# GLA first pass: two decay factors per tile computed by ScalarE alone, per head, with the reference as bias

## The chip, the cores and the metric

The kernel runs on one core of a Trainium2 chip. The metric is device time in microseconds of one execution. One execution was profiled; its own time and its span (first to last recorded instruction) are given below, beside the times of the unprofiled runs.

## The reference, cut to what matters

Two layers of a diffusion backbone over 9 tiles of 128 tokens (tile 0 is the context, tiles 1 to 8 the latent tokens), width 1024. Layer 1's mixer is a bidirectional gated linear attention with 4 heads, key width 128, value width 256. With `bc` the running sum of the log gates within a chunk, `S` the state, and everything done once forward and once backward:

```
bc = cumsum(g)                                # g = log_sigmoid(...) / 16
o  = (q * exp(bc)) @ S
o += sum_j<=i  q_i . (exp(bc_i - bc_j) * k_j)  v_j
bl = bc[last]
S  = exp(bl) * S + (k * exp(bl - bc))^T @ v
```

The factor `exp(bl - bc)` decays a token's key from its place to the end of the chunk. The backward direction has its mirror image. The kernel uses whole tiles of 128 tokens as chunks.

## The kernel before, in words

Layer 0, the MLPs and the projections are matrix products on TensorE with weights streamed in and split into two parts; they take nearly all of the span. The change lies in one stage between layer 1's input projection and its output projection: the **GLA first pass**, from about 1659 to 1813 us of the profiled span.

The stage goes through the tiles in the order `TURNS = [0, 8, 7, ..., 1]`; a **turn** is the work for one tile. The program of each engine is written out by hand in a fixed order, and an engine runs its own list strictly in order; semaphores tie the lists together. In a turn the 128x128 attention matrix of each head is built in seven **levels** (half sizes 64, 32, 16, 8, 4, 2, 1). A level needs factors `exp(difference of running sums)`:

- GpSimd (`pool_gla`) writes the differences of a level into one of three `gap` buffers (two subtractions of 128x512, lines 953 and 954; at level 6 two smaller ones).
- ScalarE (`exp_factor`) takes exponentials of it, one for the key side ("S", levels 0 to 5) and one for the query side ("M", all levels), each 128x512 for the four heads at once, into PSUM. Two PSUM banks (`E_BANK`) take the factors in turn, so the exponential of factor m waits until VectorE has used factor m-2.
- VectorE (`scale`, line 2302) multiplies keys or queries by the factor, and `place` (line 2312) puts the finished block of a level's product into the attention matrix `att`.
- TensorE multiplies (`gram`, line 2974), and in levels 2 to 5 makes the output of the turn before (`att_out`, lines 2992 and 2994), one head per level.

Three more factors per tile carry the state: `k1` and `q0` are exponentials of the running sums themselves and need no subtraction. The other two reach to the end of the tile, and these are the ones that the change touches:

- `q1` (query factor of the backward direction, tiles 8 to 1): GpSimd subtracts the tile's total `tot_b` from `bc_b` (line 945), ScalarE takes one 128x512 exponential (line 1542) into PSUM, VectorE multiplies it into `qh`. It comes at the end of a turn: on ScalarE behind `o_take` (line 1589, the copy of the previous tile's output out of PSUM), on VectorE behind `state_step` (line 2324), both of which wait for TensorE's `att_out`.
- `k0` (key factor of the forward direction, tiles 0 to 7): GpSimd subtracts the last column of `bc_f` (line 945), ScalarE takes one 128x512 exponential (`exp_keys`, line 1561) into the SBUF buffer `ek`, and GpSimd multiplies it into the keys in place (`scale_keys`, line 934). For the tile of turn n it is done in level 3 of turn n+1, behind that level's M exponential and ahead of level 4's S exponential. Tile 8 has none, so turn 2 is without it; that of the last turn's tile comes after the last turn.

On GpSimd these two subtractions take a `gap` buffer each, like the levels. `decays` (lines 1525 and 1526) makes `exp(bl)` for all tiles in two small instructions, in turn 0 at level 3.

Of the kernel before, what the change touches and what calls it, by code (L numbers as in the profile page):

```python
# [18 lines left out]
ALU = mybir.AluOpType  # L19
ACT = mybir.ActivationFunctionType  # L20
F32 = mybir.dt.float32
# [4 lines left out]
P = 128  # L26
D = 1024
DC = D // P
TILES = 9
# [14 lines left out]
GH = 4  # L44
# [4 lines left out]
GATE_NORM = 16.0  # L49
# [46 lines left out]
def build(nc, io):  # L96
# [6 lines left out]
    RK = RS + 9248  # L103

    def at(name, shape, dt, offset):
        return nc.alloc_sbuf_tensor_at(name, shape, dt, offset=offset)
# [44 lines left out]
    bc_f = at("bc_f", [P, TILES, GH, P], F32, RA)  # L151
    bc_b = at("bc_b", [P, TILES, GH, P], F32, RC)
# [83 lines left out]
    ek = at("ek", [P, GH, P], F32, RS + 4608)  # L236
    masks = at("masks", [P, len(LEVELS), P], F32, RS)
    tot_b = at("tot_b", [P, TILES, GH], F32, RS + 8704)
    dec = at("dec", [P, 2 * TILES, GH], F32, RS + 8864)
    rs4 = at("rs4", [P, TILES, 2, GH], F32, RK + 6304)  # L240

    k = RK
# [19 lines left out]
    with ExitStack() as ctx:  # L262
# [3 lines left out]
        def sem(name):  # L266
            return ctx.enter_context(nc.semaphore(name))
# [102 lines left out]
        g_sum = sem("g_sum")  # L370
        d_ready = sem("d_ready")
        e_ready = sem("e_ready")
# [27 lines left out]
        ek_ready = sem("ek_ready")  # L400
# [25 lines left out]
        TURNS = [0] + list(range(TILES - 1, 0, -1))  # L426
# [29 lines left out]
        for s in range(UNITS - CONV_UNIT):  # L456
            late_burst = s // 3 % 3 == 2
            last = s >= UNITS - CONV_UNIT - 3
# [396 lines left out]
        def key_order():  # L855

            return [tile for tile in TURNS if tile < TILES - 1]

        def factor_order():

            out = []
            for a, tile in enumerate(TURNS):
                for level in range(NL):
                    if LEVELS[level] > 1:
                        out.append(("S", tile, level))
                    out.append(("M", tile, level))
                    if level == 1 and a:
                        out += closing(TURNS[a - 1])
                    if level == 2 and tile != 1:
                        out.append(("k1", tile, 0))  # L870
                if tile:
                    out.append(("q1", tile, 0))
            return out + closing(TURNS[-1])

        factor_at = {x: i for i, x in enumerate(factor_order())}
        FACTORS = len(factor_at)

        def gap_order():

            out = []  # L880
            for a, tile in enumerate(TURNS):
                for level in range(NL):
                    out.append(("g", tile, level))
                    if level == 3 and a and TURNS[a - 1] in key_order():
                        out.append(("k0", TURNS[a - 1], 0))
                if tile:
                    out.append(("q1", tile, 0))
            out.append(("k0", TURNS[-1], 0))
            return out

        gap_at = {x: i for i, x in enumerate(gap_order())}

        def gap_user(kind, tile, level):
            if kind == "k0":
                return ek_ready, key_order().index(tile) + 1
            return e_ready, factor_at[("M" if kind == "g" else kind, tile, level)] + 1

        def gap_of(r):

            return gap[r % len(gap)]  # L900

        def plain(x):

            return x[:, 0:2, :].rearrange("p u (h n) -> p (u h) n", n=P)

        def halves(t, level):

# [17 lines left out]
        def pool_gla(pool):  # L925
            pool.wait_ge(g_sum, 2 * GH)
            pool.wait_ge(pan_used, SLOTS + FEEDS_TO_GLA - 2)
            gaps = gap_order()
            def scale_keys(tile):

                n = key_order().index(tile)
                pool.wait_ge(ek_ready, n + 1)
                pool.wait_ge(gram_ready, 8 * (TURNS.index(tile) + 1))
                nc.gpsimd.tensor_tensor(gk[:, tile], gk[:, tile], ek[:], ALU.mult).then_inc(k0_ready, 1)

            for r, (kind, tile, level) in enumerate(gaps):
                if kind == "g" and level == 6 and TURNS.index(tile) and TURNS[TURNS.index(tile) - 1] in key_order():
                    scale_keys(TURNS[TURNS.index(tile) - 1])
                if r >= len(gap):
                    pool.wait_ge(*gap_user(*gaps[r - len(gap)]))  # L940
                out = gap_of(r)
                if kind in ("k0", "q1"):
                    b = bc_b if kind == "q1" else bc_f
                    ref = tot_b[:, tile].unsqueeze(2) if kind == "q1" else b[:, tile, :, P - 1:P]
                    nc.gpsimd.tensor_tensor(plain(out), b[:, tile], ref.broadcast_to([P, GH, P]), ALU.subtract).then_inc(d_ready, 1)
                    continue
                n = LEVELS[level]
                f, b = halves(bc_f[:, tile], level), halves(bc_b[:, tile], level)
                f_ref, b_ref = f[:, :, 0, n - 1:n], b[:, :, 1, 0:1]
                x = out[:, :, :].rearrange("p u (b n) -> p b u n", n=n)  # L950
                if n > 1:
                    f_ref, b_ref = (y.unsqueeze(3).broadcast_to(f.shape) for y in (f_ref, b_ref))
                    nc.gpsimd.tensor_tensor(x[:, :, 0::2], f, f_ref, ALU.subtract)
                    nc.gpsimd.tensor_tensor(x[:, :, 1::2], b_ref, b, ALU.subtract).then_inc(d_ready, 1)
                else:
                    nc.gpsimd.tensor_tensor(x[:, :, 1, :], b_ref, b[:, :, 0, :], ALU.subtract)
                    nc.gpsimd.tensor_tensor(x[:, :, 2, :], f[:, :, 1, :], f_ref, ALU.subtract).then_inc(d_ready, 1)
            scale_keys(TURNS[-1])
# [42 lines left out]
        def _(act):  # L1001
# [11 lines left out]
            def own(ins):  # L1013
                ins.then_inc(act_own, 1)
                act.wait_ge(act_own, T.next(act_own))
# [145 lines left out]
            for u in range(UNITS):  # L1161
                p, n = divmod(u, GROUPS)
# [263 lines left out]
            for part in range(2 * 4):  # L1426
                p = part % 4
# [4 lines left out]
                g, amid, after = TURNED[part]  # L1432
# [86 lines left out]
            v_take(GROUPS - 1)  # L1519
            values_taken = [T.last(acc_read[t]) for t in range(GT)]  # L1520

            def decays():

                act.wait_ge(g_sum, 2 * GH)
                nc.scalar.activation(dec[:, 0:TILES, :], bc_f[:, :, :, P - 1], ACT.Exp, scale=1 / GATE_NORM)
                nc.scalar.activation(dec[:, TILES:2 * TILES, :], tot_b[:], ACT.Exp, scale=1 / GATE_NORM).then_inc(dec_ready, 1)

            def exp_factor(kind, tile, level=0):

                m = factor_at[(kind, tile, level)]  # L1530
                if m >= 2:
                    act.wait_ge(xt_ready, m - 1)
                else:
                    act.wait_ge(acc_read[(0, GT - 1)[m]], values_taken[(0, GT - 1)[m]])
                s = 1 / GATE_NORM
                out = factor(m)
                if kind in ("k1", "q0"):
                    nc.scalar.activation(out, (bc_b if kind == "k1" else bc_f)[:, tile], ACT.Exp, scale=s).then_inc(e_ready, 1)
                elif kind == "q1":
                    r = gap_at[(kind, tile, 0)]  # L1540
                    act.wait_ge(d_ready, r + 1)
                    nc.scalar.activation(out, plain(gap_of(r)), ACT.Exp, scale=-s).then_inc(e_ready, 1)
                else:
                    r = gap_at[("g", tile, level)]
                    act.wait_ge(d_ready, r + 1)
                    n = LEVELS[level]
                    x = gap_of(r)[:, 0::3, :] if kind == "S" else gap_of(r)[:, 1:3, :]
                    y = out.rearrange("p h (b s n) -> p s (h b) n", s=2, n=n)
                    nc.scalar.activation(y, x.rearrange("p s (b n) -> p s b n", n=n), ACT.Exp,  # L1549
                                         scale=-s if kind == "S" else s).then_inc(e_ready, 1)  # L1550

            def exp_keys(tile):

                n, r = key_order().index(tile), gap_at[("k0", tile, 0)]
                if n == 0:
                    for i in range(2):
                        act.wait_ge(og_out[i], 16 * ((TILES + 1 - i) // 2))
                else:
                    act.wait_ge(k0_ready, n)
                act.wait_ge(d_ready, r + 1)  # L1560
                nc.scalar.activation(ek[:], plain(gap_of(r)), ACT.Exp, scale=-1 / GATE_NORM).then_inc(ek_ready, 1)

            def place_wide(a, level):

# [26 lines left out]
            for a, tile in enumerate(TURNS):  # L1591
                for level in range(NL):
# [3 lines left out]
                    if level == 0:  # L1596
                        if a >= 2:
# [3 lines left out]
                                             scale=2.0).then_inc(diag_ready, 1)  # L1601
# [1517 lines left out]
```

## Time and profile before

| | us |
|---|---|
| median of 3 runs | 2732.11 |
| lowest, highest | 2731.95, 2733.51 |
| the profiled execution's own time | 2731.22 |
| its span | 2729.4 |
| TensorE busy | 2616.1 (96%) |
| VectorE busy | 1758.6 (64%) |
| ScalarE busy | 1373.6 (50%) |
| GpSimd busy | 195.6 (7%), nearly all of it in this stage |

The page's 40 slices of 68 us show TensorE at nine tenths or more in almost all of them; in the slices of the GLA stage it is at eight. The shares over the whole span say little on this stage, so it is read by itself: by windows, by GpSimd's groups of instructions, and by each engine's instructions in order of time. In the views, "idle before" is the time in which an engine stood still ahead of an instruction, with what released it. Neighbouring instructions of one form are merged in a timeline row (x2, x4). An instruction's duration is longer than its distance to the next, since two on one engine overlap a little.

### The profile page before, as it was taken

The page shows a single profiled execution, that of the slowest core. Times are in us where ns is not written, and L with a number is a line of the kernel's source. Part 1 is how long each engine was busy: PE and PEld are TensorE (multiplying, and loading weights), DVE is VectorE, ACT ScalarE, POOL GpSimd, SP SyncE. Part 2 cuts the span into 40 slices and gives each one's busy share as a digit, 9 for nine tenths or more (in the row PEclk, how much of TensorE's full clock was granted, in tenths as well). Part 3 has the DMA queues.
Part 4 walks back from the last instruction along what each step waited for, and adds up shares of the span by engine and source line. Part 5 has one row for each costly group of instructions (what it writes and reads, how often), then busy time and mean ns, then how long its engine had stood idle before and what let it go on. Part 6 is the DMA issues. An engine that isn't in the chain of part 4 may idle for free.

```text
span 2729.4 us, 37797 instructions
## 1 busy us (share of the span) xinstructions
PE 2616.1 (96%) x14547; PEld 2298.4 (84%) x14547; DVE 1758.6 (64%) x2814; ACT 1373.6 (50%) x2382; POOL 195.6 (7%) x180
## 2 busy tenths in 40 slices
PE   5999999999999999999999998889999999999998
PEld 3878888789998999788898887777899989998886
DVE  4146666564557777779822457985645577876787
ACT  5134445554444555554622677765544445554444
POOL 0000000000000000000000006982000000000000
PEclk9999999999999999999999999999999999999999
DMA  7643232644443554756523451015344444556565
GB/s 279 208 150 108 86 108 63 192 116 124 124 124 112 189 165 151 241 154 222 155 70 95 147 166 56 10 55 188 126 123 122 122 129 148 180 170 215 178 208 191
DMA packets 268606, 393.82 MB, mean 144 GB/s; under 512 B 25830, under 2 KB 207532, under 8 KB 267404
## 3 DMA queue, kind: packets, MB, share of 16 engines
q1 hardware_dynamic: 262192, 373.68, 43.5%
q10 hardware_dynamic: 4220, 9.86, 1.0%
q0 software_dynamic: 2016, 7.86, 0.8%
q8 instruction: 116, 1.90, 0.3%
q14 instruction: 62, 0.51, 0.1%
HBM read 331.98 MB, written 59.38 MB: 143 GB/s over the span
## 4 chain that ended last, share of the span: by engine, by line
PE 82%; DVE 7%; ACT 5%; DMA 3%; issue 2%; SPq 1%; POOL 1%; ACTq 0%; DVEq 0%; POOLq 0%
PE ps L2666 21%; PE ps L2779 15%; PE ps L2835 15%; PE ps L2744 9%; PE ps L2480 8%; PE ps L2870 4%; PE ps L2441 2%; PE ps L2534 2%; PE ps L2561 1%; PE ps L2497 1%; PE ps L2974 1%; ACT prT L1131 1%; SPq L659 1%; DVE t_g L1888 1%; ACT ps L1549 1%
## 5 line engine op out<-in xcount | busy, mean ns | idle before, releaser
L1693 DVE TENSOR_TENSOR p_lo<-p_raw,p_hi 128x1024 fp32r<-128x1024 f32 (+1 forms) x299 | 367.3, 1232 | 338.7 <-ACT p_hi L1042 332.4
L1042 ACT ACTIVATE p_hi<-p_raw 128x1024 fp32r<-128x1024 f32 x267 | 280.2, 1053 | 222.8 <-DMA p_raw<-mlp_w 116.2
L2835 PE MATMUL ps<-p_hi,hq_hi 128*128 128x512 f32 x672 | 209.3, 392 | 11.2 <-DVE c_sum L2046 4.6
L2835 PE MATMUL ps<-p_hi,hq_lo 128*128 128x512 f32 x672 | 207.1, 389 | 0.0
L2835 PE MATMUL ps<-p_lo,hq_hi 128*128 128x512 f32 x672 | 207.1, 389 | 0.0
L2779 PE MATMUL ps<-t_hi,w_hi 128*128 128x384 f32 x512 | 172.5, 337 | 11.1 <-DVE c_sum L2046 11.1
L2779 PE MATMUL ps<-t_hi,w_lo 128*128 128x384 f32 x512 | 172.4, 337 | 0.0
L2779 PE MATMUL ps<-t_lo,w_hi 128*128 128x384 f32 x512 | 172.2, 336 | 0.0
L2744 PE MATMUL ps<-hm_hi,p_lo 128*128 128x384 f32 x512 | 172.0, 336 | 0.0
L2744 PE MATMUL ps<-hm_hi,p_hi 128*128 128x384 f32 x512 | 171.7, 335 | 0.0
L2744 PE MATMUL ps<-hm_lo,p_hi 128*128 128x384 f32 x512 | 171.5, 335 | 0.0
L1330 ACT ACTIVATE hq_hi<-hq_raw 128x768 fp32r<-128x768 f32 x112 | 94.5, 844 | 137.7 <-DMA hq_raw<-hid_scratch 137.5
L2480 PE MATMUL ps<-h_hi,p_hi 128*128 128x384 f32 x432 | 158.5, 367 | 3.9 <-DVE h_lo L1714 3.9
L2835 PEld LDWEIGHTS ps<-p_hi,hq_hi 128*128 128x128 f32 x672 | 124.4, 188 | 41.3 <-issue 7.8
L2835 PEld LDWEIGHTS ps<-p_lo,hq_hi 128*128 128x128 f32 x672 | 126.1, 188 | 26.5
L2835 PEld LDWEIGHTS ps<-p_hi,hq_lo 128*128 128x128 f32 x672 | 126.1, 188 | 26.4
L2081 DVE TENSOR_TENSOR hq_lo<-hq_raw,hq_hi 128x768 fp32r<-128x768 f32 x112 | 107.0, 955 | 61.2 <-ACT hq_hi L1330 61.1
L2480 PE MATMUL ps<-h_hi,p_lo 128*128 128x384 f32 x432 | 145.3, 336 | 0.0
L2480 PE MATMUL ps<-h_lo,p_hi 128*128 128x384 f32 x432 | 144.9, 335 | 0.0
L2030 DVE TENSOR_TENSOR w_lo<-w_pair,w_hi 128x512 fp32r<-128x512 f32 x128 | 87.4, 685 | 65.4 <-ACT w_hi L1300 65.4
L2666 PE MATMUL ps<-p_hi,hid_hi 128*128 128x512 f32 x384 | 122.6, 400 | 3.3 <-DVE p_lo L1693 3.3
L1257 ACT ACTIVATE relu<-ps 128x384 f32<-128x384 f32 x64 | 31.5, 492 | 182.5 <-PE ps L2744 182.5
(326 smaller groups left out, 6435.8 us busy)
## 6 DMA issues: line engine op xcount, KB each, us to landing
p_raw<-mlp_w SPq DMA_DIRECT2D x208, 512.0 KB, 3.8
hq_raw<-hid_scratch SPq DMA_DIRECT2D x112, 384.0 KB, 4.2
mod_p<-mod_w SPq DMA_DIRECT2D x80, 512.0 KB, 4.0
w_pair<-mlp_w SPq DMA_DIRECT2D x32, 1024.0 KB, 5.8
p_raw<-gla_w_in SPq DMA_DIRECT2D x56, 512.0 KB, 3.5
hid_scratch<-c_out SPq DMA_DIRECT2D x128, 192.0 KB, 1.9
hid_scratch<-s_out SPq DMA_DIRECT2D x96, 192.0 KB, 2.0
p_raw<-gla_w_out SPq DMA_DIRECT2D x24, 512.0 KB, 3.6
```

What stands on the lines that cost most here:

```text
L1042: nc.scalar.activation(p_hi[s][:, :, 0:width], p_raw[s][:, :, 0:width], ACT.Copy).then_inc(pan_hi, 1)
L1330: nc.scalar.activation(hq_hi[layer][n % 4][:], hq_raw[layer][n % 4][:], ACT.Copy).then_inc(hq_rounded, 1)
L1693: V.tensor_tensor(p_lo[s][:, :, 0:width], p_raw[s][:, :, 0:width], p_hi[s][:, :, 0:width].bitcast(F32), ALU.subtract).then_inc(pan_lo, 1)
L2030: V.tensor_tensor(w_lo[layer][i][:], raw_piece(j, step), w_hi[layer][i][:].bitcast(F32), ALU.subtract).then_inc(piece_lo, 1)
L2081: V.tensor_tensor(hq_lo[layer][i][:], hq_raw[layer][i][:], hq_hi[layer][i][:].bitcast(F32), ALU.subtract).then_inc(hq_ready, 1)
L2441: return M.transpose(out, in_, ident[0:n, 0:n])
L2480: mm = M.matmul(ps[:, b, 0:GN], w[s][:, c, :], h0[n][x][:, c, :], start=(c == 0 and x == 0 and w is p_hi), stop=(c == DC - 1 and w is p_lo))
L2666: mm = M.matmul(acc(slot)[:, cols], x, flat(w[s])[:, cols], start=begin and edge == 0, stop=end and edge == 2)
L2744: mm = M.matmul(ps[:, b, 0:GN], w[s][:, c, :], x[:, c, :], start=(c == 0 and x is hi and w is p_hi), stop=(c == DC - 1 and w is p_lo))
L2779: mm = M.matmul(ps[:, c_bank(j, which), 0:GN], w[layer][i][:, c, :], second_operand(layer, step, x, c), start=(step < 3 and c == 0 and x = ...
L2835: mm = M.matmul(acc(t)[:, 512 * to:512 * (to + 1)], x[layer][n % 4][:, half, t * P:(t + 1) * P], flat(w[s])[:, 512 * half:512 * (half + 1) ...
L2870: mm = M.matmul(ps[0:width, b, 0:GN], w[s][:, c, 0:width], hx[g][x][:, c, :], start=(c == 0 and x == 0 and w is p_hi), stop=(c == DC - 1 a ...
```

## The change

The two differences disappear from GpSimd's list (and with them their turns in the ring of `gap` buffers). ScalarE reads the running sums directly and takes the exponential of each head by itself (128x128), with the reference divided by 16 as a per-partition bias. The biases stand in a small new tile `last_gap`, filled by two Copy activations and one wait of ScalarE for itself, ahead of its first exponential of the stage. So each `q1` and each `k0` factor is now four ScalarE instructions in place of one. `decays` no longer has its own wait, since the new instructions wait for the same thing earlier.

```diff
--- before.py
+++ after.py
@@ -237,6 +237,7 @@
     masks = at("masks", [P, len(LEVELS), P], F32, RS)
     tot_b = at("tot_b", [P, TILES, GH], F32, RS + 8704)
     dec = at("dec", [P, 2 * TILES, GH], F32, RS + 8864)
+    last_gap = at("last_gap", [P, 2, TILES, GH], F32, RK + 5152)
     rs4 = at("rs4", [P, TILES, 2, GH], F32, RK + 6304)
 
     k = RK
@@ -881,27 +882,16 @@
             for a, tile in enumerate(TURNS):
                 for level in range(NL):
                     out.append(("g", tile, level))
-                    if level == 3 and a and TURNS[a - 1] in key_order():
-                        out.append(("k0", TURNS[a - 1], 0))
-                if tile:
-                    out.append(("q1", tile, 0))
-            out.append(("k0", TURNS[-1], 0))
             return out
 
         gap_at = {x: i for i, x in enumerate(gap_order())}
 
         def gap_user(kind, tile, level):
-            if kind == "k0":
-                return ek_ready, key_order().index(tile) + 1
-            return e_ready, factor_at[("M" if kind == "g" else kind, tile, level)] + 1
+            return e_ready, factor_at[("M", tile, level)] + 1
 
         def gap_of(r):
 
             return gap[r % len(gap)]
-
-        def plain(x):
-
-            return x[:, 0:2, :].rearrange("p u (h n) -> p (u h) n", n=P)
 
         def halves(t, level):
 
@@ -939,11 +929,6 @@
                 if r >= len(gap):
                     pool.wait_ge(*gap_user(*gaps[r - len(gap)]))
                 out = gap_of(r)
-                if kind in ("k0", "q1"):
-                    b = bc_b if kind == "q1" else bc_f
-                    ref = tot_b[:, tile].unsqueeze(2) if kind == "q1" else b[:, tile, :, P - 1:P]
-                    nc.gpsimd.tensor_tensor(plain(out), b[:, tile], ref.broadcast_to([P, GH, P]), ALU.subtract).then_inc(d_ready, 1)
-                    continue
                 n = LEVELS[level]
                 f, b = halves(bc_f[:, tile], level), halves(bc_b[:, tile], level)
                 f_ref, b_ref = f[:, :, 0, n - 1:n], b[:, :, 1, 0:1]
@@ -1519,9 +1504,12 @@
             v_take(GROUPS - 1)
             values_taken = [T.last(acc_read[t]) for t in range(GT)]
 
+            act.wait_ge(g_sum, 2 * GH)
+            nc.scalar.activation(last_gap[:, 0], bc_f[:, :, :, P - 1], ACT.Copy, scale=1 / GATE_NORM)
+            own(nc.scalar.activation(last_gap[:, 1], tot_b[:], ACT.Copy, scale=1 / GATE_NORM))
+
             def decays():
 
-                act.wait_ge(g_sum, 2 * GH)
                 nc.scalar.activation(dec[:, 0:TILES, :], bc_f[:, :, :, P - 1], ACT.Exp, scale=1 / GATE_NORM)
                 nc.scalar.activation(dec[:, TILES:2 * TILES, :], tot_b[:], ACT.Exp, scale=1 / GATE_NORM).then_inc(dec_ready, 1)
 
@@ -1537,9 +1525,10 @@
                 if kind in ("k1", "q0"):
                     nc.scalar.activation(out, (bc_b if kind == "k1" else bc_f)[:, tile], ACT.Exp, scale=s).then_inc(e_ready, 1)
                 elif kind == "q1":
-                    r = gap_at[(kind, tile, 0)]
-                    act.wait_ge(d_ready, r + 1)
-                    nc.scalar.activation(out, plain(gap_of(r)), ACT.Exp, scale=-s).then_inc(e_ready, 1)
+                    for h in range(GH):
+                        last = nc.scalar.activation(out[:, h, :], bc_b[:, tile, h, :], ACT.Exp, scale=-s,
+                                                    bias=last_gap[:, 1, tile, h:h + 1])
+                    last.then_inc(e_ready, 1)
                 else:
                     r = gap_at[("g", tile, level)]
                     act.wait_ge(d_ready, r + 1)
@@ -1551,14 +1540,16 @@
 
             def exp_keys(tile):
 
-                n, r = key_order().index(tile), gap_at[("k0", tile, 0)]
+                n = key_order().index(tile)
                 if n == 0:
                     for i in range(2):
                         act.wait_ge(og_out[i], 16 * ((TILES + 1 - i) // 2))
                 else:
                     act.wait_ge(k0_ready, n)
-                act.wait_ge(d_ready, r + 1)
-                nc.scalar.activation(ek[:], plain(gap_of(r)), ACT.Exp, scale=-1 / GATE_NORM).then_inc(ek_ready, 1)
+                for h in range(GH):
+                    last = nc.scalar.activation(ek[:, h, :], bc_f[:, tile, h, :], ACT.Exp, scale=-1 / GATE_NORM,
+                                                bias=last_gap[:, 0, tile, h:h + 1])
+                last.then_inc(ek_ready, 1)
 
             def place_wide(a, level):
```

## Rows read from the trace of the kernel before

**Rows 1.** The page, section 4: shares of the span in the chain by engine.

```profile
PE 82%; DVE 7%; ACT 5%; DMA 3%; issue 2%; SPq 1%; POOL 1%; ACTq 0%; DVEq 0%; POOLq 0%
```

**Rows 2.** Windows: stretch, us; busy (count) PE, PEld, DVE, ACT, POOL; clock; DMA share, GB/s.

```profile
1758.90:1775.50 16.60, 13.61 (x95) 11.83 (x94) 15.64 (x27) 12.08 (x23) 16.60 (x18) 1.00 0.00 1
1780.00:1784.00 4.00, 3.95 (x17) 3.62 (x18) 3.26 (x5) 3.59 (x9) 4.00 (x5) 0.57 0.00 0
```

**Rows 3.** GpSimd groups by line: count, busy us, mean ns, idle before and its releaser.

```profile
L934 POOL TENSOR_TENSOR gk<-gk,ek 128x512 f32<-128x512 f32 x8 | 10.2, 1278 | 1.9 <-ACT ek L1561 1.9
L945 POOL TENSOR_TENSOR gap<-bc_f 128x512 f32<-128x512 f32 x8 | 8.3, 1042 | 1.0 <-ACT ps L1549 1.0
```

**Rows 4.** VectorE in order of time: start us, us, line, operation, idle before.

```profile
1694.60 0.69 DVE L2302 TENSOR_TENSOR qh<-gq,ps 128x512 f32<-128x512 f32 x1
...
1706.51 0.70 DVE L2302 TENSOR_TENSOR xx<-gq,ps 128x512 f32<-128x512 f32 x1
...
1711.02 0.69 DVE L2302 TENSOR_TENSOR qh<-gq,ps 128x512 f32<-128x512 f32 x1
...
1719.30 0.69 DVE L2302 TENSOR_TENSOR xx<-gq,ps 128x512 f32<-128x512 f32 x1
...
1720.54 0.67 DVE L2302 TENSOR_TENSOR xx<-gk,ps 128x512 f32<-128x512 f32 x1
...
1722.95 0.67 DVE L2302 TENSOR_TENSOR xx<-gq,ps 128x512 f32<-128x512 f32 x1
...
1725.74 1.65 DVE L2324 SCALAR_TENSOR_TENSOR st<-st,dec,ps 128x256 f32<-128x256 f32 x4
1727.43 0.69 DVE L2302 TENSOR_TENSOR qh<-gq,ps 128x512 f32<-128x512 f32 x1
...
1777.22 0.69 DVE L2302 TENSOR_TENSOR qh<-gq,ps 128x512 f32<-128x512 f32 x1
...
1784.64 0.74 DVE L2312 COPY_PREDICATED att<-masks,ps 128x512 f32<-128x512 int32 x1 [1.17 <-PE ps L2974]
...
1794.73 0.69 DVE L2302 TENSOR_TENSOR qh<-gq,ps 128x512 f32<-128x512 f32 x1
...
1811.32 0.69 DVE L2302 TENSOR_TENSOR qh<-gq,ps 128x512 f32<-128x512 f32 x1
```

**Rows 5.** ScalarE in order of time, the same columns.

```profile
1664.51 1.11 ACT L1549 ACTIVATE ps<-gap 128x512 f32<-128x512 f32 x2
...
1718.66 0.60 ACT L1549 ACTIVATE ps<-gap 128x512 f32<-128x512 f32 x1 [0.42 <-DVE kh L2302]
1719.29 0.63 ACT L1561 ACTIVATE ek<-gap 128x512 f32<-128x512 f32 x1
1719.83 1.10 ACT L1549 ACTIVATE ps<-gap 128x512 f32<-128x512 f32 x2
...
1725.74 1.02 ACT L1589 ACTIVATE o_b<-ps 128x1024 f32<-128x1024 f32 x1 [1.29 <-PE ps L2994]
1726.66 0.60 ACT L1542 ACTIVATE ps<-gap 128x512 f32<-128x512 f32 x1
```

**Rows 6.** ScalarE in order of time, in the attention of layer 0.

```profile
162.16 0.37 ACT L1120 ACTIVATE prob<-ps,smx 128x128 f32<-128x128 f32 x1 [1.97 <-DVE smx L1812]
162.43 0.19 ACT L1120 ACTIVATION_READ_ACCUMULATOR prob<-ps,smx 128x1 f32 x1
```

**Rows 7.** ScalarE's groups of instructions, the shapes kept apart.

```profile
L1034 ACT ACTIVATE h<-ps,mods 128x128 f32<-128x128 f32 x32 | 14.7, 458 | 38.4 <-PE ps L2441 36.9 <-DVE mods L1735 1.2 <-DVE h_lo L1714 0.3
...
L1123 ACT ACTIVATE smx<-sink,smx 128x1 f32<-128x1 f32 x72 | 20.3, 283 | 0.0
...
L1138 ACT ACTIVATE q_t<-ps 128x128 f32<-128x128 f32 x36 | 9.6, 266 | 1.2 <-PE ps L2561 1.1
...
L1120 ACT ACTIVATE prob<-ps,smx 128x128 f32<-128x128 f32 x8 | 2.9, 362 | 11.5 <-DVE smx L1812 11.5
```

**Rows 8.** The same view, 1655 to 1840 us.

```profile
L1525 ACT ACTIVATE dec<-bc_f 128x36 f32<-128x36 f32 x1 | 0.3, 263 | 0.0
```

## The prediction

> **What bounds the kernel now.** I read the chain by engine first: TensorE holds 82% of it and GpSimd 1% [rows 1]. That is a mean over stages, and in this stage it misleads, so I went on to busy time by window. In the stretch 1758.90 to 1775.50, one turn of the GLA first pass, GpSimd is busy for 16.60 of 16.60 us, VectorE for 15.64, TensorE for 13.61, ScalarE for 12.08 [rows 2]. By that view GpSimd sets the pace and the change takes the right load off. Third, the engines in order of time, to see what the pace would be without GpSimd. I measure a turn from VectorE's multiplication into `qh` (the q1 factor in use) to the next one. The marks [rows 4] give 16.42 for turn 2 (1694.60 to 1711.02), 16.41 for turn 3 (to 1727.43), 49.79 for turns 4 to 6 (to 1777.22, so 16.60 each), 17.51 for turn 7 and 16.59 for turn 8. Turn 2 has neither a k0 subtraction (1.04) nor a key multiplication (1.28) on GpSimd [rows 3]: GpSimd has some 16.60 - 1.04 - 1.28 = 14.3 us of work there, and the turn still took 16.42. So a second bound lies only 0.2 us under GpSimd's: the ring of ScalarE and VectorE, which hand each factor over two PSUM banks. Turn 3 shows it twice:
>
> - From `qh` to the M multiplication of level 5: 1722.95 - 1711.02 = 11.93 (turn 2: 1706.51 - 1694.60 = 11.91) [rows 4].
> - From there to the next `qh`: 1727.43 - 1722.95 = 4.48 [rows 4]. TensorE's `att_out` ends 2.79 after that multiplication, and releases both `o_take` on ScalarE and the state step on VectorE (both start at 1725.74) [rows 4, 5]. On VectorE the state step takes 1.69 to `qh`. On ScalarE q1's exponential starts 0.92 after `o_take` (1726.66), 3.71 after the multiplication, and its user could start 0.64 later: that is the distance from exponential to user in level 3, 1718.66 to 1719.30 [rows 4, 5]. So 3.71 + 0.64 = 4.35, under 4.48 by 0.13 only.
>
> **Part 1, GpSimd.** Each tile loses up to two subtractions of 1.04 us [rows 3], 2.1 us of 16.60 in a full turn. What this can give back is the distance to the ring's pace, 16.60 - 16.41 = 0.19 us a turn; it stands inside the sum below, since that builds new turns from turn 3's pieces, in which GpSimd costs 0.3 or less.
>
> **Part 2, the price of a small exponential.** The nearest row is the 128x128 exponential of layer 0's attention, with a per-partition bias: 362 ns [rows 7]. Its single instance lasts 0.37, and the next instruction starts 0.27 after it [rows 6]; an overlap of about 0.09. q1 goes to PSUM and I take 0.36 long, 0.27 apart. k0 goes from SBUF to SBUF: the one-element exponential with bias between SBUF tiles takes 283 ns [rows 7], and 127 more elements at (362 - 283) / 127 would add only 0.08, but that row and this differ in where they read. Where both rows exist, 512-wide exponentials take 0.63 to SBUF and 0.60 to PSUM [rows 5], so k0 gets 0.03 more: 0.39 long, 0.30 apart. Bounds: below, 266 ns, a 128x128 copy without a pointer operand [rows 7], about 0.175 apart; above, 458 ns with two pointer operands [rows 7], about 0.37 apart.
>
> The Trainium skill ("ScalarE: Activation LUTs", What ACT_TABLE_LOAD costs) says that a [128,1] pointer bias makes an activation about 280 ns + 0.833 ns per column and that neighbours overlap by about 93 ns, so four heads pay the fixed part four times: 0.387 long and 0.294 apart for 128 columns, by which the sum below would be about 8.0 instead of 7.3 (q1 0.10 more in 8 turns, k0 0.02 less in 7). The row with 0.362 stands a little under it, and I go by the row.
>
> **Part 3, k0 in level 3 (turns 1 and 3 to 8).** Before: level 3's M exponential starts at 1718.66, `ek` at 1719.29, level 4's S exponential at 1719.83, 0.54 after `ek` [rows 5]. Its user starts at 1720.54 [rows 4]; 0.64 after the exponential would be 1720.47, so the slack is 0.07. New: 4 x 0.30 = 1.20 instead of 0.54, and 1.20 - 0.54 - 0.07 = **0.59** of it delays VectorE. Behind `ek` on ScalarE stand all the later exponentials; VectorE waits for level 4's S factor, TensorE for VectorE. Nothing takes it back, as VectorE's list up to level 5 is already back to back.
>
> **Part 4, q1 at a turn's end (turns 1 to 8).** The first small exponential starts at the same 3.71. The last starts 3 x 0.27 = 0.81 later, lasts 0.36, plus 0.04 to the user: 3.71 + 1.21 = 4.92 against 4.48, **0.44** more. Next turn's S exponential starts at 3.71 + 4 x 0.27 = 4.79, its user could go at 5.43, and VectorE is at 4.92 + 0.60 anyway: no further loss.
>
> **Part 5, the first turn.** ScalarE makes the two small biases between its copy of the last value panel and the first exponential (1664.51 [rows 5]), when three gap buffers have long been filled and everyone waits for ScalarE. An instruction of this size takes 263 ns [rows 8]: about 0.17 to the next, 0.22 for the second, 0.05 for the wait on its own result: **0.44**, nothing hides it. Bounds 0.3 and 0.6.
>
> **The sum.** A full turn becomes 11.93 + 0.59 + 4.92 = 17.44. GpSimd needs 14.5 in it, so it is no bound even where `scale_keys` now gets `ek` 0.7 later. Turn 2 has no k0: 11.91 + 4.92 = 16.83. In turn 7 TensorE's granted clock was 0.57 over four microseconds [rows 2], and the placement at 1784.64 waited 1.17 for it [rows 4]; I keep 1.12 for one such drop. Turns 2 to 8: 16.83 + 6 x 17.44 + 1.12 = 122.59, against 1811.32 - 1694.60 = 116.72 [rows 4], so +5.87. Turn 1 has both places at turn 3's prices: 0.59 + 0.44 = 1.03. The first turn 0.44. Together **+7.3 us**. After the last turn k0's exponentials for tile 1 come behind q1, but TensorE first makes half of the last output; no cost. The second pass and the output projection start from the end of this stage and are shifted as a whole. Against the profiled execution, 2731.2 (span 2729.4 and 1.8 around it), that is 2738.6. The median of the runs is 0.9 above that execution: **2739.5**.
>
> With the lower price: k0 4 x 0.175 - 0.54 - 0.07 = 0.09; q1 3.71 + 3 x 0.175 + 0.27 + 0.04 = 4.54, 0.06 more. Turns 2 to 8 take 16.45 + 6 x 16.56 + 1.12 = 116.9, +0.2; with turn 1 and the start +0.8. With the upper price (k0 0.87, q1 3.71 + 1.61 = 5.32) it is +12.5.
>
> **Rivals.**
>
> - GpSimd is the only bound (turns of 16.60 with no idle time on it speak for that; turns 2 and 3 against it). Then every turn falls as far as VectorE's busy time, 15.64: 7 x 15.64 + 1.12 = 110.6, -6.1, with 0.44 at the start -5.7: 2726.4. It decides as soon as the small exponentials lie in idle time of ScalarE, of which a turn has 16.60 - 12.08 = 4.5 us. Chance 0.07.
> - The pointer operand costs nothing much and heads overlap as in the lower bound: +0.8, 2732.9. Against it: both rows with a bias are dearer than the copy. Chance 0.10.
> - Only q1 is on the path, k0 is absorbed (VectorE's later wait for TensorE or GpSimd eats it): 7.3 - 7 x 0.59 = +3.2, 2735.3. For it: turns 4 to 6 are 0.19 longer than turn 3, so some slack exists; against it, level 4's user follows without a gap. Chance 0.15.
> - Longer turns leave TensorE idle for longer at each turn's end, and its clock is granted at the lower level more often than the once of turn 7. At 1.1 us for each, two to four more give +9.5 to +11.7: 2742.7. Chance 0.13.
>
> **How the numbers follow.** The forecast has the remaining 0.55: 5.5 to 9 us more (2737.6 to 2741), by prices between 0.26 and 0.30 apart and one clock drop fewer or more. A measurement of this kernel tells some 0.2%, 5.5 us, from no change. Slower by more: the forecast (0.55), the clock rival (0.13), less a little for a low price: 0.66. Faster by more: half of the first rival's case, where the gain is nearly whole, and a little for what I don't see: 0.05. Within it: 0.29. The range leaves out the first rival and the far end of the clock's: 2732.5 to 2743.5.
>
> **What would show each step.** In the trace after: GpSimd idle for about 2.9 us of each turn, before level 6's gap (it waits for `ek`) and for free buffers; eight small exponentials per turn, 0.27 to 0.30 apart; the distance between level 3's M user and level 4's S user 1.83 (1.24 before); level 5's M user to `qh` 4.92 with VectorE idle before `qh` for ScalarE, and the state step still starting with `o_take`; turns of 17.4. The prediction is wrong if VectorE shows no idle time ahead of `qh` and of level 4's S user, or if turns come out under 16.4.

## The result and the profile after

| | us |
|---|---|
| before, median of 7 runs on the same chip (lowest, highest) | 2732.11 (2730.67, 2733.91) |
| after, median of 7 runs | 2743.29 (2740.65, 2745.4) |
| ratio after to before, 95% interval | 1.004 [1.003, 1.0049] |
| the profiled execution after: time, span | 2741.89, 2740.1 |
| after once more on another occasion (6 runs) against 22 runs of before: medians | 2740.96, 2731.76 |
| ratio there | 1.0033 [1.0021, 1.0044] |

The change makes the kernel slower, by 9 to 11 us. The forecast was 2739.5, or +7.4, with a range of 2732.5 to 2743.5; the first result lies 0.2 under the upper end of that range.

One turn after the change by window (columns as in [rows 2]): turn 4, from `qh` to `qh`.

```profile
1731.41:1748.94 17.53, 13.79 (x94) 11.92 (x94) 15.85 (x26) 13.45 (x29) 14.71 (x16) 1.00 0.00 1
```

It takes 17.53 us where the turn of [rows 2] took 16.60. GpSimd, busy for all of 16.60 then, is now idle for 2.8 us; ScalarE went from 12.08 to 13.45. No engine is full, and the turn is longer. The same turn on VectorE shows where the time sits:

```profile
1731.41 0.69 DVE L2293 TENSOR_TENSOR qh<-gq,ps 128x512 f32<-128x512 f32 x1 [0.59 <-DVE st L2315]
...
1739.69 0.69 DVE L2293 TENSOR_TENSOR xx<-gq,ps 128x512 f32<-128x512 f32 x1
...
1741.48 0.69 DVE L2293 TENSOR_TENSOR xx<-gk,ps 128x512 f32<-128x512 f32 x1 [0.46 <-ACT ps L1538]
...
1743.90 0.68 DVE L2293 TENSOR_TENSOR xx<-gq,ps 128x512 f32<-128x512 f32 x1
...
1746.70 1.66 DVE L2315 SCALAR_TENSOR_TENSOR st<-st,dec,ps 128x256 f32<-128x256 f32 x4
1748.94 0.69 DVE L2293 TENSOR_TENSOR qh<-gq,ps 128x512 f32<-128x512 f32 x1 [0.58 <-DVE st L2315]
```

Against turn 3 in [rows 4]: from level 3's M user (1739.69) to level 4's S user (1741.48) it is 1.79 in place of 1.24, with 0.46 idle for ScalarE; from level 5's M user (1743.90) to `qh` (1748.94) 5.04 in place of 4.48. The state step still starts with the output copy (1746.70 in both views), and `qh` comes 0.58 behind it; the view names the state step as releaser, but that had ended. It is the exponential on ScalarE:

```profile
1739.06 0.60 ACT L1538 ACTIVATE ps<-gap 128x512 f32<-128x512 f32 x1 [0.43 <-DVE kh L2293]
1739.69 1.28 ACT L1550 ACTIVATE ek<-bc_f,last_gap 128x128 f32<-128x128 f32 x4
1740.87 1.10 ACT L1538 ACTIVATE ps<-gap 128x512 f32<-128x512 f32 x2
...
1746.70 1.02 ACT L1580 ACTIVATE o_b<-ps 128x1024 f32<-128x1024 f32 x1 [2.08 <-PE ps L2985]
1747.62 1.23 ACT L1529 ACTIVATE ps<-bc_b,last_gap 128x128 f32<-128x128 f32 x4
```

This is the same turn on ScalarE, the answer to [rows 5]. `ek` now holds the engine for 1.18 (1739.69 to 1740.87) instead of 0.54, and q1's last exponential ends at 1748.85, 0.09 before `qh`. The small exponentials by form, after:

```profile
L1550 ACT ACTIVATE ek<-bc_f,last_gap 128x128 f32<-128x128 f32 x32 | 10.2, 389 | 0.2
L1529 ACT ACTIVATE ps<-bc_b,last_gap 128x128 f32<-128x128 f32 x32 | 9.9, 360 | 0.0
```

GpSimd's wait ahead of its key multiplication, in level 3 to 4 of turn 3, where it had none in full turns before:

```profile
1723.50 1.27 POOL L924 TENSOR_TENSOR gk<-gk,ek 128x512 f32<-128x512 f32 x1 [1.98 <-ACT ek L1550]
```

And the first turn: the two biases between the last value copy and the first exponential, which starts 1.33 after that copy began.

```profile
1664.17 1.02 ACT L1443 ACTIVATE gv<-ps 128x1024 f32<-128x1024 f32 x1 [0.33 <-PE ps L2657]
1665.09 0.26 ACT L1508 ACTIVATE last_gap<-bc_f 128x36 f32<-128x36 f32 x1
1665.24 0.22 ACT L1509 ACTIVATE last_gap<-tot_b 128x36 f32<-128x36 f32 x1
1665.50 1.12 ACT L1538 ACTIVATE ps<-gap 128x512 f32<-128x512 f32 x2
```

**Where the 10.7 us between the two profiled executions lie.** I lined up TensorE's 14547 matmuls, which are the same in both, one by one. The stage begins 0.58 later (drift of the long stage before it, which the change doesn't touch), and ends 9.65 later. From there to the end the distance varies between 7.8 and 10.9, with single stretches of lower clock in one or the other, and the spans differ by 10.7. Inside the stage: 0.41 at the start, 1.34 to the first `qh`, and turns 2 to 8 of 16.95, 17.53, 17.53, 18.43, 18.55, 17.52 and 17.54, together 124.05 against 116.72 [rows 4], so 7.33; in all 9.08. The 1.34 hold the two delays once (0.56 and 0.59) and 0.19 more in a part where both profiles show the clock at its lower level twice. Three of these turns, 5, 6 and 8, hold a drop of TensorE's granted clock (a short stretch at the lower of its two levels), which makes each 0.9 to 1.05 us longer; before, one did (turn 7, 17.51, 0.91 above the 16.60 of turns 4 to 6). One of them in the windows of the kernel after:

```profile
1752.00:1756.00 4.00, 4.00 (x21) 3.70 (x21) 3.04 (x5) 3.60 (x8) 3.95 (x5) 0.62 0.00 0
```

### The profile page after: what moved, and what is told of

Read it like the earlier page. It is cut to its first block, busy times and chain, and to the rows that moved or that the text cites. A ratio compares the mean times of both kernels' runs of the same rounds, so it can differ in the third digit from the quotient of the medians.

```text
span 2740.1 us, 37816 instructions
## 1 busy us (share of the span) xinstructions
PE 2618.3 (96%) x14547; PEld 2301.6 (84%) x14547; DVE 1759.7 (64%) x2814; ACT 1385.0 (51%) x2432; POOL 181.0 (7%) x164
## 4 chain that ended last, share of the span: by engine, by line
PE 81%; DVE 7%; ACT 5%; DMA 3%; issue 3%; SPq 1%; POOL 0%; ACTq 0%; DVEq 0%
PE ps L2657 21%; PE ps L2770 15%; PE ps L2826 14%; PE ps L2735 9%; PE ps L2471 8%; PE ps L2861 4%; PE ps L2432 2%; PE ps L2525 2%; PE ps L2552 1%; PE ps L2965 1%; PE ps L2488 1%; DMA hq_raw<-hid_scratch 1%; SPq L660 1%; ACT prT L1116 1%; DVE t_g L1879 1%
```

## The experiments

All were run with the kernel before on the same chip. "Before" is 2732.41 (33 runs) for the first four, 2732.45 (22) for the next three, 2731.76 (22) for the last three. Drops of the clock are told apart from turns by reading full turns without one.

**e1, the k0 half alone.** The kernel before with

```diff
-    gap_order: ("k0", tile, 0)
-    activation(ek[:], plain(gap_of(r)), ACT.Exp, scale=-1 / GATE_NORM)
+    for h in range(GH): activation(ek[:, h, :], bc_f[:, tile, h, :], ACT.Exp, scale=-1 / GATE_NORM, bias=last_gap[...])
```

> The kernel before, with only the k0 half of the change: GpSimd's k0 subtraction gone, four small exponentials in level 3. The theory (ScalarE and VectorE pass factors in a ring, and longer blocks on ScalarE lengthen it): distance from level 3's M user to level 4's S user 1.79 in place of 1.24, distance from level 5's M user to qh 4.48 as before, so a turn of 16.95, and +3 to +4 us in all. Rival (GpSimd is the bound): its work falls to 15.6 a turn, the turns fall with it, about -6 us. Second rival (the halves only hurt together): no change.

Measured: 2734.35, ratio 1.0011 [1.0002, 1.002]; turn 2 (no k0) 16.39, full turns 16.96 to 17.00. VectorE in one of them:

```profile
1753.65 0.69 DVE L2305 TENSOR_TENSOR xx<-gq,ps 128x512 f32<-128x512 f32 x1
...
1755.44 0.69 DVE L2305 TENSOR_TENSOR xx<-gk,ps 128x512 f32<-128x512 f32 x1 [0.46 <-ACT ps L1550]
...
1757.86 0.69 DVE L2305 TENSOR_TENSOR xx<-gq,ps 128x512 f32<-128x512 f32 x1
...
1760.67 1.66 DVE L2327 SCALAR_TENSOR_TENSOR st<-st,dec,ps 128x256 f32<-128x256 f32 x4
1762.36 0.69 DVE L2305 TENSOR_TENSOR qh<-gq,ps 128x512 f32<-128x512 f32 x1
```

1.79 from level 3 to level 4, with 0.46 of idle time for ScalarE; 4.50 from level 5's M user to `qh`, as before (4.48). The rival with GpSimd as the bound falls: GpSimd has one subtraction less and the turns are longer. The whole time, +1.9, is below the +3 to +4 expected, in part because the last turn takes 15.94, where it took 16.59 before.

**e2, the q1 half alone.** The same edit for q1 and `tot_b`, with k0 as before.

> The kernel before, with only the q1 half: GpSimd's q1 subtraction gone, four small exponentials behind the output copy at a turn's end. The theory: distance from level 5's M user to qh 5.04 in place of 4.48 to 4.70, level 3 to level 4 stays 1.24, turns of 16.95, +3.5 to +4.5 us; together with the k0 half the loss of the whole change. Rival (GpSimd is the bound): -6 us. Second rival: no change.

Measured: 2738.58, ratio 1.0022 [1.0013, 1.0031]; full turns 16.96 and 16.97.

```profile
1740.69 0.69 DVE L2305 TENSOR_TENSOR xx<-gq,ps 128x512 f32<-128x512 f32 x1
...
1741.93 0.67 DVE L2305 TENSOR_TENSOR xx<-gk,ps 128x512 f32<-128x512 f32 x1
...
1744.34 0.68 DVE L2305 TENSOR_TENSOR xx<-gq,ps 128x512 f32<-128x512 f32 x1
...
1747.14 1.65 DVE L2327 SCALAR_TENSOR_TENSOR st<-st,dec,ps 128x256 f32<-128x256 f32 x4
1749.38 0.69 DVE L2305 TENSOR_TENSOR qh<-gq,ps 128x512 f32<-128x512 f32 x1 [0.59 <-DVE st L2327]
```

The mirror image: 1.24 between the levels, 5.04 at the turn's end. The two delays are separate and add up within a turn: 16.41 + 0.55 + 0.56 = 17.52, measured 17.53. In whole times the halves are +1.9 and +6.2 by medians, where nearly equal parts were expected (+3 to +4 and +3.5 to +4.5), so both missed. Of the 4.2 between them the turns explain 0.8: e2 pays in turn 2 as well (0.55), and its last turn takes 16.21 where e1's takes 15.94. Another part is the clock: over all runs the mean granted clock was 0.9924 in e1, 0.9905 in e2 and 0.9919 in the 77 runs of before beside the experiments, and among those 77 runs a clock lower by 0.001 went with 0.8 us more. The clocks are on record to 0.001 only, so that slope is rough, and more likely too low than too high. By it the clock adds some 1.2 us to e2 and takes 0.4 from e1; the remaining 1.8 or so I can't assign.

**e3, GpSimd's relief without ScalarE's price.**

```diff
-    for h in range(GH): activation(out[:, h, :], bc_b[:, tile, h, :], ACT.Exp, scale=-s, bias=last_gap[...])
+    activation(out, bc_b[:, tile], ACT.Exp, scale=-s)      # k0 likewise, from bc_f; no last_gap
```

> Both of GpSimd's subtractions are gone, and ScalarE takes one 128x512 exponential straight from the running sums, without the reference (the two factors are then other numbers): GpSimd's relief without ScalarE's price. The theory: turns fall only to the ring's 16.4, so about 1 us less than before in all. Rival (GpSimd is the bound): turns fall to VectorE's busy time of 15.6, about -6 us.

Measured: 2731.58 (median of 11 runs; two of them took 3695 and 5975 us, and the ratio leaves those two out), ratio 0.9997 [0.9988, 1.0007]. A full turn:

```profile
1745.74:1762.14 16.40, 13.59 (x94) 11.92 (x94) 15.71 (x26) 12.17 (x23) 14.73 (x16) 1.00 0.01 1
```

16.40: the 0.19 below GpSimd's 16.60 and no more, though GpSimd is busy for only 14.73 and VectorE for 15.71. This is the ring's pace, read in the forecast from turns 2 and 3. The rival at 15.6 is out.

**e5, q1 ahead of the output copy.**

```diff
                     if level == 6 and a:
+                        exp_factor("q1", tile)
                         o_take(a - 1)
-                if tile:
-                    exp_factor("q1", tile)
```

> The changed kernel, with q1's four exponentials ahead of the output copy on ScalarE, where it stands idle for 2.08 us before each such copy. The theory: qh then waits for the state step only (4.48 after level 5's M user), turns of 16.95, about 4 us less than the changed kernel (2739). Rival (the loss at a turn's end is not q1's place on ScalarE but less work in flight on TensorE and its clock): no gain.

Measured: 2736.28, ratio 1.001 [1.0001, 1.0019]; full turns 16.96 to 16.98. ScalarE:

```profile
1744.76 0.60 ACT L1538 ACTIVATE ps<-gap 128x512 f32<-128x512 f32 x1 [0.61 <-DVE xx L2292]
1745.36 1.25 ACT L1529 ACTIVATE ps<-bc_b,last_gap 128x128 f32<-128x128 f32 x4
1747.44 1.02 ACT L1580 ACTIVATE o_b<-ps 128x1024 f32<-128x1024 f32 x1 [0.84 <-PE ps L2984]
```

VectorE around it:

```profile
1744.64 0.68 DVE L2292 TENSOR_TENSOR xx<-gq,ps 128x512 f32<-128x512 f32 x1
...
1747.44 1.66 DVE L2314 SCALAR_TENSOR_TENSOR st<-st,dec,ps 128x256 f32<-128x256 f32 x4
1749.13 0.69 DVE L2292 TENSOR_TENSOR qh<-gq,ps 128x512 f32<-128x512 f32 x1
```

The four exponentials have moved into the idle time ahead of `o_take`, and 4.49 (1744.64 to 1749.13) is back, with the state step deciding. So the loss at a turn's end was q1's place behind `o_take`, not its length as such.

**e4, the biases earlier.** The two copies go ahead of the last three value copies.

> The changed kernel, with the two bias copies ahead of ScalarE's last three value copies, where it waits for TensorE for nearly 5 us. The theory: the first S exponential comes 0.4 us earlier, nothing else changes; -0.4 us, which the times hardly show and the trace does. Rival (TensorE's first products of the stage or the gaps set the start): no change in the trace either.

Measured: 2741.3, ratio 1.003 [1.0018, 1.0042]. ScalarE:

```profile
1659.43 0.27 ACT L1505 ACTIVATE last_gap<-bc_f 128x36 f32<-128x36 f32 x1 [3.09 <-DVE tot_b L2249]
...
1664.24 1.02 ACT L1443 ACTIVATE gv<-ps 128x1024 f32<-128x1024 f32 x1 [0.33 <-PE ps L2656]
1665.16 1.11 ACT L1537 ACTIVATE ps<-gap 128x512 f32<-128x512 f32 x2
```

The first exponential starts 0.92 after the last value copy began, 0.41 sooner than in the changed kernel (1.33), as expected; the change in the whole time is too small to be told from the runs' scatter.

**e6, all three moved.** e4 and e5 together, and k0's heads behind level 5's M exponential and ahead of q1's. Since `ek` is complete later, GpSimd's multiplication of `ek` into the keys moves as well, from level 6 to level 2 of the turn after. ScalarE's part of the diff:

```diff
-                    if level == 3 and a and TURNS[a - 1] in key_order():
-                        exp_keys(TURNS[a - 1])
+                    if level == 5 and a and TURNS[a - 1] in key_order():
+                        exp_keys(TURNS[a - 1], range(0, 2))
                     if level == 6 and a:
+                        if TURNS[a - 1] in key_order():
+                            exp_keys(TURNS[a - 1], range(2, GH))
+                        exp_factor("q1", tile)
                         o_take(a - 1)
```

> The changed kernel with its exponentials where ScalarE is idle: the biases ahead of the last value copies, q1 ahead of the output copy, k0's heads 0 and 1 behind level 5's M exponential and heads 2 and 3 behind level 6's; GpSimd multiplies k0 into the keys at level 2 of the turn after. The theory: both added waits go, turns of 16.4, 8 to 9 us less than the changed kernel and about 1 us less than the kernel before (2731). Rival (the ring gives back only q1's part, and k0's shows up as a later output copy): turns of 16.9, about 2736.

Measured: 2730.17, ratio 0.9993 [0.9984, 1.0001]. ScalarE between level 5 and the output copy, and the turn by window:

```profile
1737.71 0.69 ACT L1552 ACTIVATE ek<-bc_f,last_gap 128x128 f32<-128x128 f32 x2
1738.31 0.58 ACT L1538 ACTIVATE ps<-gap 128x512 f32<-128x512 f32 x1
1738.83 0.68 ACT L1552 ACTIVATE ek<-bc_f,last_gap 128x128 f32<-128x128 f32 x2
1739.41 1.23 ACT L1529 ACTIVATE ps<-bc_b,last_gap 128x128 f32<-128x128 f32 x4
1740.97 1.02 ACT L1583 ACTIVATE o_b<-ps 128x1024 f32<-128x1024 f32 x1 [0.33 <-PE ps L2989]
```

```profile
1742.66:1759.07 16.41, 13.59 (x94) 11.92 (x94) 15.74 (x26) 13.56 (x28) 14.80 (x16) 1.00 0.01 1
```

All eight small exponentials stand where ScalarE was idle: two ahead of level 6's M exponential, which waited 0.61 for VectorE in e5, and six ahead of the output copy, where 0.33 of the wait are left. The turn is 16.41, the ring's pace, with ScalarE's busy time (13.56) no less than in the changed kernel (13.45). That GpSimd's multiplication moved too is no part of the gain as far as e3 shows: there it stood at level 6, and the turns were 16.40. It beats the changed kernel by 11 to 13 us, and the kernel before by 2 us in the median, which its interval just fails to tell from none.

**e7, the small exponentials without the bias operand.** Diff: `bias=last_gap[...]` is left out in both places, the copies stay. The kernel thus leaves out the reference, and the two factors are other numbers, as in e3.

> The changed kernel without the bias operand in the small exponentials (the reference is left out, so the two factors are other numbers): four exponentials per factor with immediate operands. It splits the price into the number of instructions and the pointer. If the pointer is most of it: small exponentials 0.27 long and 0.18 apart, a block of 0.7 to 0.8, turns of 16.6 and about 2734. If the number of instructions is most of it: blocks stay over 1.0 us, turns over 17.2, above 2740.

Measured: 2735.05, ratio 1.001 [1.0001, 1.0019]; full turns 16.79 to 16.81. The forms:

```profile
L1549 ACT ACTIVATE ek<-bc_f 128x128 f32<-128x128 f32 x32 | 7.3, 297 | 0.2
L1529 ACT ACTIVATE ps<-bc_b 128x128 f32<-128x128 f32 x32 | 6.9, 272 | 0.0
```

The pointer makes 0.09 of each instruction, 389 - 297 and 360 - 272. Of the 1.12 that the change adds to the ring's 16.41, it makes 17.53 - 16.80 = 0.73 a turn, about 8 x 0.09; the 0.39 left are the three more instructions per factor.

**e8, the state step spread (on top of e6).** VectorE multiplies `qh` first, and the state step's heads go behind level 0's S and M users of the next turn.

```diff
                     scale("S", tile, level)
+                    if level == 0 and a > 1: state_step(1, TURNS[a - 2], (0, 1))
                     scale("M", tile, level)
+                    if level == 0 and a > 1: state_step(1, TURNS[a - 2], (2, 3))
...
-                    state_step(1, TURNS[a - 1])
+                    dve.wait_ge(upd_ready, a)
                     scale("q1", tile)
```

> The version with q1, k0 and the biases moved into ScalarE's idle time, and in addition VectorE multiplies qh before the state step, whose four heads go into the next turn, two behind level 0's S user and two behind its M user. The theory (with GpSimd relieved and ScalarE's blocks out of the way the ring is the bound, and it loses about 1 us per turn to VectorE's waits for factors, which the state step can fill): turns of 15.4 to 15.7, about 6 us less than with the state step in place, 2724. Rival (TensorE or GpSimd is next, at 16.4): no gain over 2730.

Measured: 2733.81, ratio 1.001 [1.0001, 1.0019]; full turns 16.89 to 16.91. A miss: slower than e6 by 3.6 us, or 4.3 with each taken against the runs of before beside it. ScalarE, then VectorE:

```profile
1746.15 1.02 ACT L1583 ACTIVATE o_b<-ps 128x1024 f32<-128x1024 f32 x1 [0.33 <-PE ps L2996]
1747.07 1.11 ACT L1538 ACTIVATE ps<-gap 128x512 f32<-128x512 f32 x2
1748.93 0.60 ACT L1594 ACTIVATE att<-ps 128x512 f32<-128x512 f32 x1 [0.75 <-PE ps L2976]
...
1749.90 1.12 ACT L1538 ACTIVATE ps<-gap 128x512 f32<-128x512 f32 x2
```

```profile
1746.25 0.69 DVE L2297 TENSOR_TENSOR qh<-gq,ps 128x512 f32<-128x512 f32 x1 [0.21 <-PE ps L2996]
1747.70 0.69 DVE L2297 TENSOR_TENSOR xx<-gk,ps 128x512 f32<-128x512 f32 x1 [0.76 <-ACT ps L1538]
...
1751.20 0.67 DVE L2297 TENSOR_TENSOR xx<-gk,ps 128x512 f32<-128x512 f32 x1
```

VectorE waits 0.76 for level 0's S factor, whose exponential stands behind `o_take` (0.92) on ScalarE. The state step had been the cover for that copy; taken away, the copy is what VectorE waits for, and behind it ScalarE waits for TensorE's first product (0.75 ahead of 1748.93), which it doesn't in e6. `qh` comes 1.6 us sooner than in e6, but from `qh` to level 1's S user it is 4.95 (1746.25 to 1751.20) in place of 2.85: 0.5 us lost in all, as 16.90 against 16.41. `qh` still waits for TensorE (0.21), as the edit keeps that wait ahead of it. So the work was already hiding another wait. This is read from the two traces; no run moves the copy alone.

**e9, the same order with GpSimd loaded.** The kernel before, q1's one exponential ahead of `o_take`, state step spread as in e8.

> The kernel before with GpSimd's two subtractions kept, q1's single exponential ahead of the output copy, and the state step spread as in the other version. The theory: GpSimd's 16.6 of work per turn holds every full turn, so turns stay at 16.6 and the total within 1 us of before; the relief of GpSimd is worth something only together with the other moves. Rival (the order on VectorE and ScalarE is all): it gains the same 6 us.

Measured: 2736.43, ratio 1.0015 [1.0006, 1.0024]; full turns 17.11 to 17.13. Neither was right, since the spread costs here too. e9 and e8 differ in more than GpSimd's load (k0's place, the small exponentials), so 17.12 against 16.90 doesn't isolate it. But e9's own turn 3 takes 16.90 as well, and in its window GpSimd has little work, 14.49 us against 16.63 in the full turns:

```profile
1714.51:1731.41 16.90, 13.58 (x94) 12.00 (x93) 15.62 (x26) 12.17 (x23) 14.49 (x16) 1.00 0.00 0
```

GpSimd's load is worth 0.22 a turn here, close to e3's 0.19.

**e10, the changed kernel again.**

> The changed kernel once more, beside the two others on one chip, to size its loss: the terms read from its stage give 7.3 as forecast; 9 us were read from its first trace with two extra stretches of TensorE at the lower clock. Expected 8 to 11 us over the kernel before, turns of 17.53 without a drop of the clock, 16.5 for the last turn.

Measured: 2740.96, ratio 1.0033 [1.0021, 1.0044]; turns 16.94, 17.54, 17.53, 18.6 (a drop of the clock), 17.50, 17.53 and 16.50.

## Why the prediction was right, and what it had wrong

- **The bound.** Right. GpSimd was full and still only 0.19 above the next bound. e3 took GpSimd's load off by itself and got turns of 16.40, and e1 and e2 each took half of it off and got longer turns. One reading behind it was wrong: turn 2 has a short list on GpSimd (14.3), but in turn 2's window GpSimd was busy for 16.32 of 16.42 us, since its list does not run in step with VectorE's. Its light window is turn 3, and the ring's pace rested on that turn. Turns 2 and 3 before:

```profile
1694.60:1711.02 16.42, 13.64 (x95) 11.94 (x94) 15.71 (x27) 11.89 (x22) 16.32 (x18) 1.00 0.27 98
1711.02:1727.43 16.41, 13.59 (x94) 11.92 (x94) 15.68 (x27) 12.09 (x23) 15.26 (x16) 1.00 0.00 0
```

- **Price of the small exponentials.** 0.389 and 0.360 long were forecast as 0.39 and 0.36. The distances were 0.30 and 0.27 forecast, 0.295 (1.18 / 4) and 0.29 measured: so q1's was 0.02 too short: I had taken the overlap of layer 0's row, where the instruction behind is of another kind. The distance of 0.294 that follows from the Trainium skill ("ScalarE: Activation LUTs", What ACT_TABLE_LOAD costs) is met by both, its length of 0.387 by k0 only (0.389; q1 0.360). That page of the Trainium skill says that each pointer operand adds about 93 ns; the traces agree with 92 and 88 (e7). Its estimate for q1, 0.44 + 0.10 = 0.54, was the better one: 0.56 was measured.
- **k0 in level 3.** 0.59 forecast, 1.79 - 1.24 = 0.55 measured, in e1 by itself.
- **q1 at a turn's end.** 0.44 forecast, 5.04 - 4.48 = 0.56 measured (1748.94 - 1747.62 = 1.32 from the first small exponential to its user, 1.21 forecast: 3 x 0.02 by the distances and 0.05 from the last exponential's end to its user).
- **The start.** 0.44 forecast, 0.41 measured, and e4 takes it away.
- **The last turn.** The step "turns 2 to 8: 6 x 17.44" was wrong for turn 8. Tile 1 has no k1 factor, so its turn is shorter on VectorE: 16.50 in e10, 15.64 in e6. Before, it took 16.59, and with GpSimd's load off (e3) 15.67, so GpSimd's list had hidden that. This is 0.94 too much in the sum; by chance q1's 0.12 too little in 8 turns offsets it.
- **The sum without drops of the clock.** 0.41 + 1.15 (turn 1) + 0.53 + 1.12 + 0.97 + 0.91 + 0.93 + 0.92 (turn 7, against the 16.60 beside it, the drop of before taken out) - 0.09 = 6.9; forecast 7.3. The same sum from e10's profile is 6.9 too. The forecast took 1.12 for one drop; it was 0.91 before and 0.9 to 1.05 in the three turns after.
- **The clock.** A rival of its own with two to four drops more. In the profiled execution it came true: two more in the stage (0.90 + 1.02 + 1.04 - 0.91 = 2.05 us), so with 0.19 before the first `qh` 6.9 + 2.05 + 0.19 = 9.1, the stage's 9.1. In e10's profile the turns held one, as before, and one more stood right behind the last turn, where the profile before has none. From the last `qh` to the second pass's first product of `st` and `gq`, before and then e10:

```profile
1811.32:1819.30 7.98, 6.59 (x36) 5.88 (x37) 2.80 (x5) 3.71 (x10) 2.13 (x2) 1.00 0.57 199
1819.40:1829.06 9.66, 8.27 (x36) 7.12 (x37) 2.92 (x5) 4.64 (x13) 2.13 (x2) 0.82 0.47 163
```

It cost 1.68 there. The clock thus takes about 2 us in both profiles of the changed kernel. But there is one profile of before, and e1, e2, e4, e6, e7 and e9 have this last drop too, so its tie to the change is not shown. Over 13 runs of the changed kernel the mean granted clock was 0.9914, against 0.9919; by the rough 0.8 us per 0.001 above that is 0.4 us. So more drops are a part of the loss, and how large a one is not settled.

- **What stays open.** The means of all runs lie 9.9 us apart (2742.06 over 13, 2732.19 over 77). The mechanism has 6.9, the clock by that count 0.4. Some 2.5 us are not explained. They could be the 2 us of drops that both profiles show; the profiled pair also has 0.58 before the stage and 1.0 behind it, where the two programs do the same. That the first result, +11.2, stayed in a range that ends at +11.4 is in part luck: the forecast's sum has 7.3, and it took more drops of the clock for a rival with a chance of 0.13.

## What to carry to other kernels

An engine that is busy without a gap is the bound only as far as the next one allows: look for a turn in which it happened to have less to do, and see whether that turn was shorter. Splitting one instruction into four on an engine with idle time costs nothing where it stands in that time and most of its price where another engine waits behind it: here the same eight instructions cost 1.12 us a turn in one place (the changed kernel) and nothing in another (e6). And before taking work away from in front of a wait, ask what else it is covering (e8).

## What the runs showed that I had not expected

- The order on ScalarE matters more than its load: e6 has 13.56 us of ScalarE work in a turn of 16.41, the changed kernel 13.45 in 17.53.
- One drop of TensorE's clock costs a turn of this stage 0.9 to 1.1 us, although TensorE is idle for 3 to 4 us of each turn, and 1.7 us right behind the last turn (e10). The longest idle stretch, 2.39 us in turn 5, lies right behind `qh`; the drops of turns 5, 6 and 8 began 2.7 to 4.2 us behind such a `qh`, and so came when it was over or nearly so. That this is why so little of a drop is hidden is my reading; no run tests it.
- The changed kernel's profile and e10's have their drops in different turns with the same code; differences of 1 to 2 us between single executions say nothing about a change here.
